# The first mixer's input projection: pairs of tiles from seven products of quarters

## The reference

```
lat = split_cols(u_lat @ w_in, EVEN_SPLITS)
ctx = split_cols(u_ctx @ w_in, EVEN_SPLITS)
# EVEN_SPLITS = (1536: q, k, v of the recurrence; 512: its gate; 16 and 16: decay and strength;
#                256: low-rank query; 128: low-rank key and value; 32: rotary key)
qkv = silu(short_conv(qkv, conv_w))          # five taps along the tokens
q = l2_normalize(q) * GDN_DK ** -0.5         # by heads of 64
k = l2_normalize(k)
g = -exp(a_log) * softplus(a + dt_bias)
...                                          # chunked recurrence over the tokens, in both directions
o = rms_norm(o) * silu(gate)                 # and low-rank attention beside it
```

## Time and profile before

| what | value |
|---|---|
| median of 3 runs | 2145.39 us (2144.38 to 2149.76) |
| profiled execution | 2145.4 us |
| its span, first to last instruction | 2143.6 us |
| TensorE busy | 2083.7 us (97%) |
| VectorE busy | 1261.6 us (59%) |
| ScalarE, GpSimd busy | 509.8 us (24%), 188.4 us (9%) |
| transfers | 289.96 MB, 135 GB/s on the mean |

### The profile page before, as it was taken

One profiled execution on the slowest core, in us unless ns is written; L12 is line 12 of the kernel. 1 busy time (PEld: TensorE's weight loads), 2 busy tenths in 40 slices (PEclk: granted clock), 3 DMA queues, 4 the chain that ended last, 5 costly groups with the idle time before them and its releaser, 6 DMA issues.

```text
span 2143.6 us, 34632 instructions
## 1 busy us (share of the span) xinstructions
PE 2083.7 (97%) x14684; PEld 1468.0 (68%) x14684; DVE 1261.6 (59%) x2175; ACT 509.8 (24%) x1060; POOL 188.4 (9%) x179
## 2 busy tenths in 40 slices
PE   8999989999999999999999999999999999999999
PEld 4446656454888884466467994686895488769646
DVE  2674445677554547552356775685786528678743
ACT  2434332543100000131252100223310122421101
POOL 0004333000000000021100000002121000202100
PEclk9999999999999999999999999999999999999999
DMA  8121455205322224454103445333344443234442
GB/s 358 62 79 63 157 201 212 96 33 221 122 97 79 98 79 163 171 138 137 59 2 138 173 162 176 148 118 118 146 170 176 162 147 124 99 138 165 171 175 79
DMA packets 41721, 289.96 MB, mean 135 GB/s; under 512 B 5088, under 2 KB 6496, under 8 KB 7264
## 3 DMA queue, kind: packets, MB, share of 16 engines
q1 hardware_dynamic: 39392, 279.99, 35.6%
q0 software_dynamic: 1312, 3.15, 1.1%
q10 hardware_dynamic: 864, 4.61, 0.5%
HBM read 286.15 MB, written 1.05 MB: 134 GB/s over the span
## 4 chain that ended last, share of the span: by engine, by line
PE 87%; DVE 8%; ACT 2%; issue 2%; DMA 1%; ACTq 0%; POOL 0%; DVEq 0%
PE banks L1036 23%; PE banks L1564 15%; PE banks L1845 12%; PE banks L2356 6%; PE banks L3021 5%; PE banks L3314 3%; PE banks L417 3%; PE banks L644 2%; PE banks L816 2%; PE banks L455 1%; PE banks L831 1%; PE banks L2061 1%; PE banks L2044 1%; PE banks L822 1%; PE banks L852 1%
## 5 line engine op out<-in xcount | busy, mean ns | idle before, releaser
L1036 PE MATMUL banks<-arena 128*128 128x512 f32 x392 | 186.2, 593 | 0.7 <-DVE arena L1901 0.5
L1036 PE MATMUL banks<-weight_ring,arena 128*128 128x512 f32 x338 | 156.8, 593 | 0.0
L1036 PEld LDWEIGHTS banks<-arena 128*128 128x128 f32 x392 | 74.0, 190 | 93.8 <-issue 92.4
L1564 PE MATMUL banks<-normed,weight_ring 128*128 128x128 f32 x1040 | 130.8, 276 | 2.3 <-ACT normed L575 1.2
L2356 PE MATMUL banks<-normed,weight_ring 128*128 128x512 f32 x288 | 126.1, 593 | 0.0
L1564 PEld LDWEIGHTS banks<-normed,weight_ring 128*128 128x128 f32 x1040 | 123.2, 192 | 3.7 <-issue 2.9
L1001 DVE TENSOR_TENSOR arena<-weight_ring 128x512 f32<-128x512 f32 x67 | 46.2, 690 | 130.9 <-PE banks L1036 130.8
L1564 PE MATMUL banks<-normed,arena 128*128 128x128 f32 x960 | 116.4, 275 | 2.1 <-DVE arena L1530 2.1
L1036 PEld LDWEIGHTS banks<-weight_ring,arena 128*128 128x128 f32 x338 | 63.5, 190 | 76.5 <-issue 75.7
L1564 PEld LDWEIGHTS banks<-normed,arena 128*128 128x128 f32 x960 | 111.5, 192 | 2.9 <-DVE arena L1530 2.9
L3021 PE MATMUL banks<-normed,weight_ring 128*128 128x256 f32 x448 | 102.8, 390 | 0.0
(11 more groups left out here) (545 smaller groups left out, 3977.3 us busy)
## 6 DMA issues: line engine op xcount, KB each, us to landing
weight_ring<-in_weights SPq DMA_DIRECT2D x266, 1024.0 KB, 4.8
residual<-in_tokens ACTq DMA_DIRECT2D x1, 2048.0 KB, 15.0
mix<-in_rpb POOLq DMA_DIRECT2D x32, 64.0 KB, 3.6
constants<-in_const ACTq DMA_DIRECT2D x1, 1953.5 KB, 11.7
out<-residual SPq DMA_DIRECT2D x4, 256.0 KB, 2.4
branch<-arena POOLq DMA_DIRECT2D x1, 512.0 KB, 4.9
normed<-in_ple POOLq DMA_DIRECT2D x1, 512.0 KB, 3.5
vector_params<-in_vectors ACTq DMA_DIRECT2D x1, 223.0 KB, 5.7
```

The costliest lines, as they stand in the source:

```text
L1036: return pe.matmul(self.bank[i], left, b, start=(p == 0), stop=(p == n - 1))
L1564: mm = pe.matmul(o, a[:, k * P:k * P + P], right[:, k], start=(k == 0), stop=(k == H - 1))
```

## The change

Sixteen of the nineteen tiles (q, k, v, low-rank query, and the gate's second and third) are made in eight pairs. A pair's weights are one chunk: four quarters of 128 x 512 (quarter 0 and 1: first half of the features for the first and the second tile; 2 and 3: second half). The token columns are split into context and tokens, the features into halves; a pair's eight quarter results come from seven products of quarters, each 4 matmuls of 128x256, and sums of them (`quarter_product`, `combine`). Some results come out with the sign turned, and the Silu or the multiplication that follows turns it back.

Three of the seven need sums of weights and four need sums of tokens. The token sums are made once, by VectorE (`add_tokens`). Of the weight sums GpSimd makes all but one by transfers from memory, some with `accum_op=ALU.add`, into three buffers in turn and into the chunk itself; VectorE makes the last one (`last_sum`). ScalarE copies three quarter results per pair out of the banks (`keep`, `first_quarter`). Tiles 15, 14 and 18 stay single products; 15 now comes first, 14 after the pairs, 18 as before inside the recurrence. The low-rank and gate tiles' later steps stand behind the pairs on every engine, and `ready` now also waits for the last pair.

The core of the diff (setup, names and buffers cut):

```diff
+EVEN_PAIRS = [(0, 1), (2, 3), (4, 5), (6, 7), (8, 9), (10, 11), (12, 13), (16, 17)]
...
-    out.append(pack_tiles(x["w_in_even"][0], even_in_columns()))
+    out += [pack_tiles(x["w_in_even"][0], tiles[:1]), pick([15]), quarters(pick(sum(EVEN_PAIRS, ())), KT).reshape(-1, P, P), pick([14, 18])]
...
+        def quarter_product(p, i):
+            x, y = pair_banks(p)
+            o = {1: halves_of(x)[:, 0], 2: halves_of(x)[:, 0], 6: halves_of(x)[:, 1], 5: halves_of(y)[:, 0], 3: halves_of(y)[:, 0], 7: halves_of(y)[:, 1], 4: halves_of(y)[:, 1]}[i]
+            right = {1: u[:, 0:H, 0:S], 2: u[:, H:, 0:S], 3: u[:, H:, S:], 4: t4, 5: t1, 6: t2, 7: t3}[i]
+            left = quarter(p, {1: 0, 5: 1, 2: 2, 4: 3}[i]) if i in (1, 2, 4, 5) else last_sums[p % 3] if i == 3 else weight_sums[p % 3][:, {7: 0, 6: 1}[i]]
+            for k in range(H):
+                mm = pe.matmul(o, left[:, k * P:k * P + P], right[:, k], start=(k == 0 and i in (1, 5)), stop=(k == H - 1), skip_group_check=True)
+            return mm
+
+        def pair(p):
+            made = sg["f_products"].sem
+            K.arrived(pe, pair_first[p])
+            hit(pe, "f_quarters", p - 1)
+            quarter_product(p, 1).then_inc(made, 1)
+            sums_added(pe, 4 * p + 3)
+            if p == 0:
+                hit(pe, "f_tokens", 4)
+            quarter_product(p, 5)
+            quarter_product(p, 7).then_inc(made, 1)
+            hit(pe, "f_first", 3 * p + 1)
+            sums_added(pe, min(4 * p + 5, 4 * NP))
+            quarter_product(p, 6)
+            quarter_product(p, 2).then_inc(made, 1)
+            hit(pe, "f_first", 3 * p + 2)
+            hit(pe, "f_weights", p + 1)
+            quarter_product(p, 3)
+            quarter_product(p, 4).then_inc(made, 1)
...
+        project(0)
+        for p in range(NP):
+            if p == 1:
+                hit(pe, "e_taken", 1)
+            pair(p)
+            if p == 0:
                 key_rows()
                 cumulate()
+            if 2 <= p <= 5:
+                unit_sum(2 * p - 4)
+                unit_sum(2 * p - 3)
+        turn(0)
+        turn(1)
+        project(1)
+        turn(2)
+        turn(3)
+        low_rank(0)
+        low_rank(1)
+        for i in range(4, 8):
+            turn(i)
...
+        def add_tokens():
...
+            dve.tensor_tensor(out=t3, in0=u[:, H:, S:], in1=u[:, 0:H, S:], op=ALU.subtract).then_inc(added.sem, 1)
...
+        def last_sum(p):
+            sums_added(dve, min(4 * p + 5, 4 * NP))
...
+            dve.tensor_tensor(out=last_sums[p % 3], in0=quarter(p, 2), in1=weight_sums[p % 3][:, 1], op=ALU.add).then_inc(sg["f_weights"].sem, 1)
+
+        def combine(p):
+            x, y = pair_banks(p)
+            first, o = kept[p % 2], target(p)
+            hit(dve, "f_first", 3 * p + 3)
+            step(dve.tensor_tensor(out=partial[:, 0], in0=first[:, 0], in1=halves_of(x)[:, 1], op=ALU.add))
+            step(dve.tensor_tensor(out=partial[:, 1], in0=partial[:, 0], in1=first[:, 2], op=ALU.add))
...
+            dve.tensor_tensor(out=o[:, 3], in0=partial[:, 1], in1=first[:, 1], op=ALU.add)
+            hit(dve, "f_products", 4 * p + 4)
+            dve.tensor_tensor(out=o[:, 1:3], in0=bc(partial[:, 0], 1, 2), in1=halves_of(y), op=ALU.add).then_inc(sg["f_quarters"].sem, 1)
...
+        for p, units in ((2, ()), (3, (0,)), (4, (1,)), (5, (2, 3))):
+            last_sum(p + 1)
+            combine(p)
+            convolve(2 * p)
+            convolve(2 * p + 1)
+            for i in units:
+                unit(i)
+        last_sum(7)
+        combine(6)
+        unit(4)
+        unit(5)
+        combine(7)
+        unit(6)
         unit(7)
         low_rank(0)
         low_rank(1)
...
+        for p in range(NP + 1):
+            if p < NP:
+                c = pair_first[p] // CB
+                pool.wait_ge(K.chunk_arrived[c % RING].sem, 16 * (c // RING + 1))
+                hit(pool, "f_products", 4 * (p - 2))
+                pool.dma_start(weight_sums[p % 3], source(p, 1, 2)).then_inc(summed.sem, 16)
+            if p > 0:
+                pool.dma_start(weight_sums[(p - 1) % 3][:, 1], source(p - 1, 3), accum_op=ALU.add).then_inc(summed.sem, 16)
+            if p < NP:
+                sums_added(pool, 4 * p + 1)
+                pool.dma_start(weight_sums[p % 3], source(p, 0, 2), accum_op=ALU.add).then_inc(summed.sem, 16)
+                pool.dma_start(quarter(p, 1), source(p, 3), accum_op=ALU.add).then_inc(summed.sem, 16)
+                sums_added(pool, 4 * p + 3)
...
-    ready = [(sg[n], at[n] + counts[n]) for n in ("e_last", "e_factors", "e_key", "e_unit", "e_turn_out")]
+    ready = [(sg[n], at[n] + counts[n]) for n in ("e_last", "e_factors", "e_key", "e_unit", "e_turn_out", "f_quarters")]
```

More of the change, by code:

```diff
@@ L2330, in even_projections @@
     gates_first = K.next_blocks(KT, (sg["e_gates"], at["e_gates"] + 1))
-    first = [K.next_blocks(KT, (sg["e_product"], at["e_product"] + f + 1)) for f in range(NF)]
+    first = [K.next_blocks(KT, (sg["e_product"], at["e_product"] + 1))]
+    pair_first = [K.next_blocks(CB, (sg["f_products"], at["f_products"] + 4 * p + 4)) for p in range(NP)]
+    assert not pair_first[0] % CB
+    first += [K.next_blocks(KT, (sg["e_product"], at["e_product"] + f + 1)) for f in (1, 2)]
+    single_bank = (2, 0, 2)
     ab = K.bank(7, 384).rearrange("p (t n) -> p t n", t=4)
@@ new lines, in scalar @@
+        turn_out(0)
+        turn_out(1)
+        take(1)
+        hit(act, "e_sum", 8)
+        hit(act, "e_taken", 2)
+        hit(act, "f_quarters", 7)
+        hit(act, "f_first", 3 * 6 + 3)
+        act.activation(K.square, qd, ACT.Square).then_inc(sg["e_low_square"].sem, 1)
+        act.activation(low_squares, kvd[:, 0, :], ACT.Square).then_inc(sg["e_low_square"].sem, 1)
+        turn_out(2)
+        turn_out(3)
+        act.wait_ge(sg["e_unit"].sem, at["e_unit"] + 8)
+        for i in range(2):
+            act.wait_ge(sg["e_low_sum"].sem, at["e_low_sum"] + i + 1)
+            act.activation(roots[i], K.bank(4 + i), ACT.Sqrt, bias=K.c("eps"), scale=1.0 / (256, 128)[i]).then_inc(sg["e_low_root"].sem, 1)
@@ L2563, in vector @@
         ins.then_inc(sg["e_last"].sem, 1)
-        for m in range(5, 12):
-            convolve(m)
-            unit(m - 5)
+        for p, units in ((2, ()), (3, (0,)), (4, (1,)), (5, (2, 3))):
[11 more added lines that the diff above has]
+        unit(6)
         unit(7)
@@ L2590, in even_projections @@
+        act.activation(gate[:, 3, :], K.bank(single_bank[2]), ACT.Silu).then_inc(sg["e_taken"].sem, 1)
+    last = {"product": last_product, "take": last_taken, "taken": [(sg["e_taken"], at["e_taken"] + NS)],
+            "others_taken": [(sg["e_taken"], at["e_taken"] + 2), (sg["f_quarters"], at["f_quarters"] + NP)]}
+    ready = [(sg[n], at[n] + counts[n]) for n in ("e_last", "e_factors", "e_key", "e_unit", "e_turn_out", "f_quarters")]
     return ready, [(sg["e_low"], at["e_low"] + 2)], last
```

202 lines of the change are left out of this document (118 added, 84 removed).

## The result

The changed kernel takes **2180.31 us** (median of four runs, 2178.46 to 2186.27), the kernel before 2147.26 beside it: a ratio of 1.0168, 95% interval 1.0151 to 1.0185. It is slower by 1.7%, outside the range of the prediction, in the direction of its first rival. The profiled execution took 2180.81.

The account below looks back on a forecast made before the run. TensorE, busy 97% of the span, was taken as the bound. Passes saved, first wait, late recurrence start, low-rank scaling and clock summed as -13.1 + 3.5 + 4.6 + 3.0 + 1.7 = -0.3, giving 2145.1 us, range 2136 to 2167.

Parts of the forecast that it names:

- first rival: Waits for accumulated sums in the pairs: GpSimd's round is the bound, change slower, 2158 at 15.5 us a round; chance 0.31.
- GpSimd's chain of transfers: Two dependent transfer steps for each pair's weight sums: 11.8 us a round, hidden behind TensorE's products, no cost.
- limit of 13.6: Seven rounds must fit in 95 us of the pairs; above 13.6 us a round, each us costs seven.
- upper bound of 15.4: GpSimd's round if accumulations read twice at the slower rate and the pair's chunk gets in between: 15.4 us.
- lower bound: GpSimd's round if accumulating is as cheap as a copy: steps of 4.1 and 4.7, 8.8 us a pair.
- The rule on half the rate: Adding transfers run at about half a copy's rate: GpSimd's round 11.2 us without the chunk, 13.7 with it.
- The clock: TensorE's clock may fall to 1.2 GHz around two waits: 0 to 6.8 us lost, taken as 1.7.
- The saving of the passes: A pair takes 12.10 us of TensorE instead of 13.74; over eight pairs 13.1 us saved.
- The first wait: TensorE waits near 51 us for the token sums, 3.5 us, including 1.8 for constants delayed by GpSimd's transfers.
- The schedule of pairs: TensorE's pairs at 12.1 to 13.8 us each, pair 1 starting at 67.4 and pair 7 ending at 158.9.
- VectorE's lag: VectorE needs 17.9 us a pair and falls behind; unit lengths left for the end delay the recurrence by 4.6 us.
- low-rank scaling on VectorE: At the recurrence's start this work delays VectorE's first subtraction: a loss of 0 to 3 us, taken as 3.0.

Follow-up runs that it names:

- experiment 1: The changed kernel without GpSimd's weight-sum transfers and the waits for them, products reading unsummed quarters, VectorE's last sum kept: 2149.71 us, ratio 1.0014.
- experiment 2: The changed kernel with the same transfers, order and waits, but each only copies and none adds: 2160.78 us, ratio 1.0086.
- experiment 3: The changed kernel with the next pair's copy issued behind this pair's accumulations, so GpSimd waits for transfers once a round: 2175.39 us, ratio 1.0138.
- 7: The changed kernel filled up to 512 TensorE instructions more than before ahead of the recurrence, giving the block ends of before: 2172.1 us, ratio 1.0133.
- 9: The kernel of experiment 4 with its waits taken out by reordering and earlier unit lengths, filled up to 512 instructions: 2135.14 us, ratio 0.9959.
- 10: The same kernel as 9, but filled up to 472 instructions, which is 216 modulo 256: 2129.14 us, ratio 0.9932.
- experiment 4: The changed kernel with all four weight sums of a pair made by GpSimd's own additions, no transfers, no VectorE last sum: 2155.65 us, ratio 1.0041.
- Experiment 8: The kernel of experiment 1 filled up to 512 TensorE instructions more than before ahead of the recurrence: 2140.62 us, ratio 0.9987.
- 18 cuts: The kernel before with 18 of the stage's matmuls cut into halves of 256 columns, 72 instructions more: 2158.29 us, ratio 1.0066.
- 54 cuts: The kernel before with 54 of the stage's matmuls cut into halves of 256 columns, 216 instructions more: 2139.74 us, ratio 0.9971.
- 36 cuts: The kernel before with 36 of the stage's matmuls cut into halves of 256 columns, 144 instructions more: 2152.91 us, ratio 1.0035.

## Why the prediction was wrong

**The failed step: GpSimd's chain of transfers.** The prediction took the round as 11.8 us, under a limit of 13.6 below which "this chain costs nothing", and so its sum has no term for it. The round took 17.3, beyond the upper bound of 15.4, and TensorE lost 31.3 us in the pairs. The limit was right in size (13.4 us a pair in experiment 1): at 14.6 (experiment 2) TensorE waits 5.7 us in all for the sums, at 15.4 (experiment 3) 12.1, at 17.3 19.3. What failed is the price of a step. The steps were priced by the earlier trace rows, single transfers of 3.5 and 4.9 us, and by 425 GB/s, the rate of other queues in the earlier trace rows. In experiment 2's chain of waits, where the transfers only copy, the landings alone take longer:

```profile
100.28 6.47 DMA mix<-in_weights
...
107.74 5.48 DMA weight_ring<-in_weights
```

With what stands ahead of them the two steps take 7.5 (99.58 to 107.04) and 6.5 us (to 113.50), where the prediction's lower bound had 4.1 and 4.7; with adding they take 8.8 and 7.9 (the chain above). Of the 8.5 us by which the round exceeds that lower bound of 8.8, 5.8 are there without any adding and 2.7 come with it. So the larger part isn't the adding, which the prediction doubted, but plain transfers issued two at a time, which it thought it knew. Why those are slow stays open.

The rule on half the rate from the Trainium skill (Collectives: The Full Stack, section The bandwidth ceiling: the fold count and why AG ≠ RS ≠ AR) would have given 11.2 to 13.7, too short as well, for it says nothing on the copies. Here 12.6 MB, two thirds of them added, ran at 11.0 in place of 14.7 GB/s an engine; half the rate for the added two thirds would have made it 8.8.

**The clock.** Taken as 1.7 us, bounds 0 to 6.8 for two waits. It fell in or behind waits of 2.2 to 5.0 us in the pairs and of 3.5 in the tail, not at all of them, and made TensorE's passes 7.6 us longer in the pairs. That follows from the first miss, and most of it cost no time of its own, since every pair waits for the end of a round in any case.

**Rival 1.** Its mechanism decided, in its place. At its price of 7 us for each us above 13.6, 17.3 would give 25.9; between the first and the last wait for the sums the rounds cost 24.7. The other 6.6 us of the pairs lie ahead of the first wait and behind the last.

**Not foreseen: the block ends,** 8.9 of the 35.4 us at the end. With them put back (7) the changed kernel is still 1.3% slower: the transfers decide, the block ends add.

**What held.** The saving of the passes: 13.1 forecast; in experiment 1 the recurrence starts 6.5 earlier with 5.6 us of waits that weren't there before, so 12.1. The first wait: 3.5 forecast, 3.3 measured, and 1.8 without the transfers, where the prediction had 1.7: so they did cost it 1.5 (taken as 1.8): the last constants are there at 49.39 us in place of 48.13. The schedule of pairs and VectorE's lag: the recurrence was due at 176.4 and starts at 175.2 in experiment 1; from the last product of a pair to the recurrence 17.5 were forecast, 17.4 measured.

**What was over-counted.** The 3.0 us of low-rank scaling on VectorE. In the changed kernel no wait of TensorE at the start of the recurrence comes of it, nor in 7, 9 and 10. In experiments 1, 4 and 8 one does: in 8 VectorE's first subtraction begins 7.0 us after the recurrence (3.0 before), and behind it TensorE waits for GpSimd (the same in 1 and 4):

```profile
PE banks L2007 <- POOL mix L2222: 1.4, 2, 0.9
```

So of the 3.0 at most 1.4 weren't hidden. For a kernel without rounds, which has neither the 1.8 us of the constants nor the 1.7 of the clock, the prediction's terms give -3.8 with the 3.0 and -6.8 without. Experiment 8's recurrence starts 6.4 earlier than before; its time is 3.5 less (2140.62 against 2144.07), by the interval between 6 less and equal, and so can't tell the two sums apart.

The sum as it was, by the start of the recurrence: -6.5 (experiment 1) + 31.3 in the pairs + 3.4 tail - 0.1 = +28.1; then +8.9 in the recurrence and -1.5 behind it: 35.4, of a span from 2143.6 to 2179.0.

## What to carry to other kernels

Price a chain of dependent transfers by transfers issued the way the chain issues them (here two at a time from GpSimd), not by a single one or by another queue's rate, and take every step from issue to landing; whether the transfers add was the smaller question here. When a chain sets the pace, don't add up idle time and a lower clock as two losses: the engine that waits has time to spare. Where an engine is nearly idle and the data are already on the chip, let it do the additions, but start it where it doesn't disturb its neighbour. And when a change adds instructions ahead of a stage dense in small matmuls, compare that stage before and after on its own: here it moved by up to 16 us with the instruction count modulo 256, more than the change itself could gain, and an experiment that alters the count must be read with that in mind.

## What the runs showed of the hardware that wasn't expected

- TensorE's code arrives in blocks of 16,384 bytes (119 in the changed kernel), 255 records apart in the recurrence, and TensorE stands still for up to 3.6 us around some of them (18 cuts) and goes on 1.2 to 1.6 us after the block has landed. The Trainium skill (Advanced Engine Details and Errata, section ISA Cache) states cache lines of 16 KB, 256 instructions; the trace agrees. No run here shows how far ahead of its use a block is asked for.
- Behind such gaps the granted clock falls too: 0.51 for 7 us in the earlier trace rows; in the recurrence with 54 cuts it is 1.00 on the mean, with 36 cuts 0.97.
- Two transfers of GpSimd's queue under way together moved 154 GB/s while no other queue had a packet (experiment 2, 115.5 to 118 us); a single one moved 284 (before, 1365.6 to 1367.4 us).
- Additions on GpSimd slow some of VectorE's: 5.78 for 3.11 us in experiment 4. The Trainium skill (GPSIMD Engine Reference, section 1. Specifications) states that GpSimd's interfaces to the on-chip memory are shared with VectorE, in contention with instructions of two such inputs; the row agrees.
- Kernels with the same number modulo 256 as the changed one (146) had recurrences from 199.6 (experiment 2) to 207.1 us (experiment 3), so the block ends don't fix the time alone. What else moves it stays open.
